# Sums of squares in four column groups, roots and inverses on 128 partitions, in a hybrid decoder step

## The reference, cut to what matters

```python
q = l2_normalize(q.reshape(n_b, t_len, H_C, DK)) * (DK ** -0.5)   # x * rsqrt(sum(x*x) + 1e-6)
k = l2_normalize(k.reshape(n_b, t_len, H_C, DK))
...
o, delta_new = gated_delta_rule(q, k, v, g, beta, delta_prev)      # chunks of tokens, four heads
o = rms_norm(o, o_norm_g) * silu(c_gate)
y_c = o.reshape(n_b, t_len, D_C)
x = x + einsum('bte,ed->btd', concatenate([y_a, y_b, y_c]), w_out)
x = x + hier_moe(rms_norm(x, norm2_g), ...)                        # 32 experts of 256
```

## Time and profile before

| | |
|---|---|
| runs | 720.87 us median of 3 (718.63, 720.87, 726.35) |
| span of the profiled execution | 720.5 us, 0.4 us under the median |
| its busy shares | PE 89%, PEld 64%, DVE 49%, ACT 28%, POOL 18% |
| chain that ended last | PE 68%, DMA 18%, DVE 8%, ACT 2%, issue 2% |
| mean granted TensorE clock | 0.971 |

### The profile page before, as it was taken

The page is one execution under the profiler, slowest core; times in us unless marked ns, Lnnn a source line. Parts: engine busy times, 40 slices in busy tenths (PEclk is TensorE's granted clock), DMA queues, the critical chain, the costliest instruction groups (busy, mean ns, idle before and its releaser), DMA issues.

```text
span 720.5 us, 12831 instructions
## 1 busy us (share of the span) xinstructions
PE 644.8 (89%) x4674; PEld 463.6 (64%) x4675; DVE 355.3 (49%) x705; ACT 200.9 (28%) x419; POOL 129.0 (18%) x226
## 2 busy tenths in 40 slices
PE   5998999999979998999999999787887799789885
PEld 4998998889869888894455655343343455455431
DVE  4657686879987748645765551111111112111237
ACT  6464366531432351234021201111111111101114
POOL 0010010200530010040011235311122223223110
PEclk9999999999989999999999979999999999999996
DMA  9232333233090000005961168999999999989836
GB/s 280 64 90 60 87 88 88 60 89 71 6 365 10 1 1 1 2 1 190 346 210 58 65 253 310 411 411 413 416 415 414 407 409 412 415 347 395 323 108 268
DMA packets 74792, 150.60 MB, mean 209 GB/s; under 512 B 14964, under 2 KB 51144, under 8 KB 66543
## 3 DMA queue, kind: packets, MB, share of 16 engines
q1 hardware_dynamic: 69167, 141.28, 53.1%
q0 software_dynamic: 5568, 8.54, 3.3%
HBM read 140.90 MB, written 18.20 MB: 221 GB/s over the span
## 4 chain that ended last, share of the span: by engine, by line
PE 68%; DMA 18%; DVE 8%; issue 2%; ACT 2%; SPq 0%; POOLq 0%; DVEq 0%; POOL 0%; ACTq 0%
PE ps L1899 21%; DMA wd<-w_down 17%; PE ps L2255 14%; PE ps L1994 8%; PE ps L2086 7%; DVE XX L1581 2%; PE ps L2207 2%; PE ps L2277 1%; PE ps L2296 1%; PE ps L2176 1%; PE ps L1912 1%; PE ps L1848 1%; DMA yk<-expert_rows 1%; PE ps L1988 1%; PE ps L2064 1%
## 5 line engine op out<-in xcount | busy, mean ns | idle before, releaser
L2255 PE MATMUL ps<-gu,xT 128*64 128x256 f32 x992 | 123.0, 392 | 35.2 <-DMA wd<-w_down 32.2
L1899 PE MATMUL ps<-hhi,whi 128*128 128x256 f32 (+1 forms) x416 | 121.1, 291 | 3.4 <-DVE wlo L1281 1.8
L2255 PEld LDWEIGHTS ps<-gu,xT 128*64 128x64 f32 x992 | 68.8, 139 | 85.4 <-issue 36.8
L1899 PE MATMUL ps<-hlo,whi 128*128 128x256 f32 (+1 forms) x416 | 118.8, 286 | 0.0
L1899 PE MATMUL ps<-hhi,wlo 128*128 128x256 f32 (+1 forms) x416 | 118.8, 286 | 0.0
L1760 DVE SCALAR_TENSOR_TENSOR gact<-gth,ps 128x128 f32<-128x128 f32 x32 | 9.2, 288 | 156.5 <-ACT gth L1013 156.5
L1899 PEld LDWEIGHTS ps<-hhi,whi 128*128 128x128 f32 x416 | 79.7, 192 | 7.9 <-issue 4.6
L1899 PEld LDWEIGHTS ps<-hhi,wlo 128*128 128x128 f32 x416 | 80.1, 192 | 0.0
L1899 PEld LDWEIGHTS ps<-hlo,whi 128*128 128x128 f32 x416 | 79.8, 192 | 0.0
L2255 PE MATMUL ps<-wd,aT 128*64 128x512 f32 x248 | 59.4, 600 | 0.0
L2086 PE MATMUL ps<-wout,yT 128*128 128x512 f32 x128 | 59.1, 602 | 0.0
(11 more groups left out here) (405 smaller groups left out, 979.9 us busy)
## 6 DMA issues: line engine op xcount, KB each, us to landing
gu<-w_gate SPq DMA_DIRECT2D x31, 1024.0 KB, 11.3
gu<-w_up SPq DMA_DIRECT2D x31, 1024.0 KB, 14.4
wd<-w_down SPq DMA_DIRECT2D x31, 1024.0 KB, 17.2
wraw<-w_in SPq DMA_DIRECT2D x26, 512.0 KB, 3.8
wout<-w_out SPq DMA_DIRECT2D x1, 4096.0 KB
yk<-expert_rows SPq DMA_DIRECT2D x8, 512.0 KB, 6.9
x<-x_prompt SPq DMA_DIRECT2D x4, 512.0 KB, 7.1
s<-state_delta SPq DMA_DIRECT2D x4, 512.0 KB, 6.2
```

The costliest lines, as they stand in the source:

```text
L1899: last = mm(ps[:, 2 * (n % 2) + half, 0:hi - lo], weights[:, c, :], h[:, c, lo:hi], start=c == 0 and j == 0, stop=c == KT - 1 and j == len ...
L2255: last = mm(ps[g * CAP:(g + 1) * CAP, bank, 0:width], left(c), right(c, g), start=c == 0, stop=c == steps - 1)
```

## The change

The sum over partitions is taken in quarters of the columns. Quarter g of a tile (136 columns, 130 for the outputs) goes to column group g, that is to PSUM partitions 32g to 32g+31, with a stationary operand of 128x32 that has ones in columns m and m+16. Each sum so stands twice in its group of 32 partitions, at m and at m+16. Root and inverse then run on 128 partitions and a quarter of the columns, and the split is one `scalar_tensor_tensor`: a column `low` (0 for the first 16 partitions of each 32, -1 for the others) leaves the rounded inverse in the first and makes the rest in the second. The spread picks a row and its rest with a 128x128 operand out of `quarter_sel`, one matmul for each quarter. The constants grow by 37 columns, which the same DMA loads; a fill of `norm` with zeros (line 1318) goes and a copy of 16 columns comes in its place.

```diff
-            return cst[:, C_COL + 7 - m:C_COL + 15 - m]
+            return cst[:, C_COL + 3 - m:C_COL + 35 - m]
+        def select_quarter(g, m):
+            return quarter_sel[:, 4 * g + m:4 * g + m + 1].broadcast_to([P, P])
...
-                copy(rn[:, 0, :], ps[0:8, 4, 0:HC], ACT.Sqrt, scale=0.25,
-                     bias=epsc[0:8, :]).then_inc(sums_ready, 1)
+                copy(rn[:, 0, :], ps[:, 4, 0:QC], ACT.Sqrt, scale=0.25, bias=epsc[:, :]).then_inc(sums_ready, 1)
...
-            link(nc.vector.memset(norm[:, :].bitcast(F32), 0.0))
+            link(nc.vector.tensor_copy(quarter_sel[:, :], cst[:, C_QUARTERS:C_QUARTERS + 16]))
...
                 link(nc.vector.reciprocal(rn[:, 1, :], rn[:, 0, :]))
-                link(nc.vector.tensor_copy(norm[0:8, :], rn[:, 1, :]))
-                nc.vector.tensor_tensor(norm[32:40, :], rn[:, 1, :], norm[0:8, :], ALU.subtract).then_inc(norms_ready, 1)
+                link(nc.vector.tensor_copy(norm[:, :], rn[:, 1, :]))
+                stt(out=norm[:, :], in0=norm[:, :], scalar=low, in1=rn[:, 1, :], op0=ALU.mult, op1=ALU.add).then_inc(norms_ready, 1)
...
-                for half in range(2):
-                    last = mm(ps[0:8, 4, 0:HC], column(j % 4 + 4 * half), sq[j % 2][:, half * HC:(half + 1) * HC],
-                              start=j % 4 == 0 and half == 0, stop=j % 4 == 3 and half == 1)
+                for g in range(4):
+                    last = mm(ps[32 * g:32 * g + 32, 4, 0:QC], column(j % 4), sq[j % 2][:, g * QC:(g + 1) * QC],
+                              start=j % 4 == 0, stop=j % 4 == 3)
...
-                for half in range(2):
-                    last = mm(ps[:, 6 + half, 0:HC], select(j % 4 + 4 * half), norm[:, :], start=True, stop=True)
+                for g in range(4):
+                    last = mm(ps[:, 6 + g // 2, g % 2 * QC:(g % 2 + 1) * QC], select_quarter(g, j % 4), norm[:, :], start=True,
+                              stop=True)
```

More of the change, by code:

```diff
@@ L42 @@
 HC = CV // 2
+QC = CV // 4
+QT = T // 4
 EPS = 1e-6
@@ L75 @@
 C_COL = C_LM + 128 * LEVELS
-C_REV = C_COL + 16
+C_REV = C_COL + 36
 C_GIR = C_REV + NE
@@ L84 @@
 C_PICK = C_CAPS + MORE
-C_END = C_PICK + 8
+C_QUARTERS = C_PICK + 8
+C_LOW = C_QUARTERS + 16
+C_END = C_LOW + 1
 def constants():
@@ L99, in constants @@
         c[:, C_LM + n * P:C_LM + (n + 1) * P] = (i // 2 == j // 2) & (i % 2 == 1) & (j % 2 == 0)
-    c[:, C_COL + 7] = 1.0
+    c[:, C_COL + 3] = 1.0
+    c[:, C_COL + 3 + 16] = 1.0
     c[:, C_REV:C_REV + NE] = 99 - np.arange(NE)
@@ L111, in constants @@
     c[:, C_PICK:C_PICK + 8] = p[:, None] % 32 == np.arange(8)
+    for g in range(4):
+        for r in range(4):
+            c[:, C_QUARTERS + 4 * g + r] = (p // 32 == g) & (p % 16 == r)
+    c[:, C_LOW] = -1.0 * (p % 32 >= 16)
     return c
@@ L190, in build @@
         sel = keep("sel", [40, 8], F32R)
-        norm = keep("norm", [40, HC], F32R)
+        quarter_sel = keep("quarter_sel", [P, 16], F32R)
+        norm = keep("norm", [P, QC], F32R)
         rowsr = keep("rowsr", [40, SEQ], F32R)
@@ L248, in build @@
         uas = first("uas", [P, 2, NS, WA])
-        rn = first("rn", [8, 2, HC])
+        rn = first("rn", [P, 2, QC])
         delta = Region(K4, K5 - 1920)
@@ L274, in build @@
         osq = [mix(f"osq{s}", [P, T]) for s in range(2)]
-        rno = mix("rno", [8, 2, HT])
+        rno = mix("rno", [P, 2, QT])
         rowq2 = mix("rowq2", [27, CQ * P])
@@ L344, in column @@
         def column(m):
-            return cst[:, C_COL + 7 - m:C_COL + 15 - m]
+            return cst[:, C_COL + 3 - m:C_COL + 35 - m]
         def select(m):
             return sel[:, m:m + 1].broadcast_to([40, P])
+        def select_quarter(g, m):
+            return quarter_sel[:, 4 * g + m:4 * g + m + 1].broadcast_to([P, P])
+        low = cst[:, C_LOW:C_LOW + 1]
         def rows(i):
@@ L917, in _ @@
             act.wait_ge(onorm_done, H)
-            copy(rno[:, 0, :], ps[0:8, 1, 0:HT], ACT.Sqrt, scale=1.0 / P,
-                 bias=epsc[0:8, :]).then_inc(oroot_ready, 1)
+            copy(rno[:, 0, :], ps[:, 1, 0:QT], ACT.Sqrt, scale=1.0 / P, bias=epsc[:, :]).then_inc(oroot_ready, 1)
             act.wait_ge(rows_turned, 4)
@@ L1602, in _ @@
             link(nc.vector.reciprocal(rno[:, 1, :], rno[:, 0, :]))
-            link(nc.vector.tensor_copy(norm[0:8, 0:HT], rno[:, 1, :]))
-            tt(norm[32:40, 0:HT], rno[:, 1, :], norm[0:8, 0:HT], ALU.subtract).then_inc(onorm_ready, 1)
+            link(nc.vector.tensor_copy(norm[:, 0:QT], rno[:, 1, :]))
+            stt(out=norm[:, 0:QT], in0=norm[:, 0:QT], scalar=low, in1=rno[:, 1, :], op0=ALU.mult, op1=ALU.add).then_inc(onorm_ready, 1)
             vec.wait_ge(ds_vec, 8)
@@ L2106, in _ @@
                 pe.wait_ge(osq_ready, n + 1)
-                for half in range(2):
-                    last = mm(ps[0:8, 1, 0:HT], column(n + H * half), osq[n % 2][:, half * HT:(half + 1) * HT],
-                              start=n == 0 and half == 0, stop=n == H - 1 and half == 1)
+                for g in range(4):
+                    last = mm(ps[32 * g:32 * g + 32, 1, 0:QT], column(n), osq[n % 2][:, g * QT:(g + 1) * QT], start=n == 0,
+                              stop=n == H - 1)
                 last.then_inc(onorm_done, 1)
@@ L2128, in _ @@
                     pe.wait_ge(oscaled, n - 1)
-                for half in range(2):
-                    last = mm(ps[:, (0, 4)[n % 2] + half, 0:HT], select(n + H * half), norm[:, 0:HT], start=True, stop=True)
+                for g in range(4):
+                    last = mm(ps[:, (0, 4)[n % 2] + g // 2, g % 2 * QT:(g % 2 + 1) * QT], select_quarter(g, n), norm[:, 0:QT],
+                              start=True, stop=True)
                 last.then_inc(onorm_done, 1)
```

## The result

| | median (us) | range, runs | ratio to before, 95% |
|---|---|---|---|
| before | 721.66 | 718.63 to 726.35, 4 | |
| changed | 710.50 | 709.71 to 710.75, 4 | 0.9852 [0.982, 0.9883] |

The change makes the kernel 1.5% faster, 11.2 us by the medians. The profiled execution of the changed kernel took 710.75 us with a span of 708.9. An execution thus takes 1.8 us more than its span.

The account below looks back on a forecast made before the run. TensorE was taken to bound the projection. Savings of 5.7 us there and 1.9 in the norm of the outputs, 7.6 in all, took 720.5 to 712.9, given as 713.2 us; range 711.0 to 718.0.

Parts of the forecast that it names:

- What bounds the kernel: Projection, 73 to 196 us: TensorE alone, busy 35.00 of 35 us, so sums and spreads between tiles are paid in full.
- The new sum: Sums of squares: eight passes of 136 columns in four column groups take 0.37 us instead of 1.02, saving 0.65 each.
- The new spread: Spreads in the projection: four 128-row matmuls take 0.47 us instead of 0.59, saving 0.12 alone, 0.62 together with a sum.
- The ways in and out: Around a spread: leaving and re-entering the full array costs 0.35 us, expected to go with all 128 rows in use.
- Cover by DVE: End of projection: DVE's inversion saves 0.8 us, and its 1.16 us wait at the last gate remains as cover.
- The outputs: Norm of the outputs: first spread 1.3 us earlier, outer products a further 0.6, together 1.9 us saved.
- the term for the half-clock stretches: Between stages: granted clock may fall elsewhere, a microsecond or two either way; inside the gain-caught-later rival, 715.2 us, chance 0.14.
- narrow float32r: Rival, spreads: float32r at 136 columns runs like plain float32, a spread costs 0.93 us; time 718.9 us, chance 0.12.
- the ways don't stay: Rival, spreads: the ways in and out stay, a spread costs 0.82 us; time 717.6 us, chance 0.10.
- the loads don't hide behind the streaming: Rival, spreads: four weight loads hide behind streaming, 0.25 us in all; time 711.4 us, chance 0.06.
- the groups share: Rival, sums: column groups do not overlap, a sum takes 1.76 us instead of 1.02; time 728.6 us, chance 0.03.
- the gain isn't caught by DVE: Rival, projection: DVE uses only its 2.88 us idle and the shorter inversion, projection gives 3.7; 715.2 us, chance 0.14.

Follow-up runs that it names:

- the two experiments in which the trace names DVE as what it waited for: Kernel before with only the spreads' operands brought to 128 rows, 718.75 us; changed kernel with each reciprocal of q and k done twice, 711.43 us.
- the 128-row experiment: Kernel before with only the spreads' operands brought from 40 to 128 rows, sums, roots and inverses as they were: 718.75 us, ratio 0.9961.

## Why the prediction was wrong by a little, step by step

**What bounds the kernel** was right: TensorE in the projection, busy 35.00 of 35 us before and after, so that every sum and spread is paid in full.

**The new sum**, 0.37 predicted, 0.37 measured. The estimate from the experts' four groups holds: eight passes in two rounds. A repeat behind another sum costs 0.23, the estimate without the ways 0.25.

**The new spread** is the term that was mis-sized. A tile with a spread alone takes 158.89 - 152.71 = 6.18 where it took 6.37, so a spread saves 0.19 and not 0.12; at the fifth of the eight spreads, where the step was 6.48 before, it saves 0.30. The projection gave 6.14 instead of 5.7. Both prices were off. The old one was read too low: the 28.89 us of 240 matmuls hold a first tile of 5.86, behind other matmuls, and run to the end of the last one; between its like a tile takes 5.74 from start to start and not 5.78, so the old spread cost 0.63 and not 0.59. The new one costs 6.18 - 5.74 = 0.44 and not 0.47. Its weight loads start 0.11 apart, close to the 0.106 of the earlier trace rows. The second matmul starts only 0.06 behind the first, which makes the 0.40 from start to start above, but most of that is given back where the second projection matmul behind a spread starts 0.17 behind the first and not 0.12. The row of the routing has the same cheap first step, 0.03, and 0.11 for each later one; its mean of 0.106 hides that. Behind a sum the spread saved what was predicted: 7.39 - 6.77 = 0.62. The 81 ns of the Trainium skill ("TensorE: Matmul & The Clock Gate", "Back-to-back issue gap") would make 0.32 of four, as an estimate; the run has 0.44, so the measured 0.11 a load was the better price.

**The ways in and out** go, as predicted, but not wholly: the first projection matmul behind a spread lasts 0.33, where 0.28 was foreseen. The 128-row operands alone take 6.37 - 6.01 = 0.36 from a spread, the 0.35 read from the earlier trace rows. The rule of the Trainium skill ("TensorEngine Tiling (Array Packing)", "Key Properties"), that a change of the tiling mode drains TensorE, agrees with this.

**Cover by DVE.** The inversion got shorter by 2.6 - 1.6 = 1.0 us, 0.8 predicted (6.1 ns a column for the reciprocal, not 5.3), and the wait at the last gate was 1.05 where 1.16 was foreseen. But the statement that those 1.16 are the cover was wrong: the nearer edge is the spread of the fifth tile, with 0.45 after the change. In the kernel before it had none. There the chain that ended last and DVE's timeline have

```profile
164.96 0.07 issue
165.02 0.49 PE ps L1923 x2
...
164.16 0.71 DVE L1423 SCALAR_TENSOR_TENSOR cv<-cv,ps 128x544 f32<-128x544 f32 x1
```

The spread starts 0.15 behind the end of DVE's multiplication at 164.87, as it does in the two experiments in which the trace names DVE as what it waited for. This is the 0.11 by which the step with the fifth spread was longer, 6.48 for 6.37. The prediction looked for waits of DVE, and this is a wait for DVE.

**The outputs**, 1.9 predicted, 2.18 measured. The first spread moved by 1.63, since besides the sums (3.73 to 2.35) ACT's shorter root, 0.37 instead of 0.47, stands ahead of its copy of the turned rows, and the first spread no longer waits for DVE's inversion. Before, it did:

```profile
334.18 0.29 PEld L2130 LDWEIGHTS ps<-norm,sel 40*128 40x128 f32 x2 [0.27 <-DVE norm L1604]
```

The rest of the 2.18 is 0.55, predicted 0.6. PE no longer holds DVE, as predicted. One sign was wrong: the outer products are still released by ACT's copy, which ends at 331.52, 0.1 after DVE's last multiplication.

**The time and the range.** The terms were 0.7 us too small in all (0.4 in the spreads, 0.3 in the outputs), and that leaves 712.5, inside the range. The step that failed is the term for the half-clock stretches. The prediction has it among the rivals, "Where PE idles between stages the granted clock may also fall at other points than now, a microsecond or two either way", but prices it with one value above the forecast and gives it nothing in the lower end of a range that "reaches from 711.0 to 718.0". As a scatter about every case it reaches well below 711: the same kernel was timed from 708.01 to 715.73, the stretch up to the eighth tile alone differing by 3.0 us and the one up to the first expert by 2.7. That the first four fell just below 711.0 is in part luck, since the two repeats of the same kernel have medians of 714.74 and 711.34, both inside the range. Within 1% had more of the chance than faster, though 8.3 us alone are 1.15%; the forecast itself was 1.06%. The note that the profiled execution lies 0.4 under the median set a span against times; it had 722.46 us of its own, 0.8 over the median of the four. That error cost little here, and 712.9 with 0.4 is 713.3, not 713.2.

**The rivals** fell by the trace: narrow float32r runs at the price of its loads, the ways don't stay, the loads don't hide behind the streaming (0.11 from one to the next), the groups share, and the gain isn't caught by DVE. This last one was nearer than its 0.14 says: the 128-row experiment is that case, and without the shorter inversion the change would have lost 0.58.

## What to carry to other kernels

A wait that is cover must be looked for at every place where the slower engine hands something back, not only at the last one: here the bound would have moved at a spread that waits for the multiplication of the tile before, with 0.45 us to spare against 1.05 at the end, and with none before the change. Such a place shows on the engine that waits, in one step that is longer than its like (6.48 among four of 6.37). Narrow matmuls in a row paid for their weight loads here, 0.11 us each. The price of a plain tile is read from start to start between its like, not from the mean of a stretch whose ends cost extra. And where stages differ by a microsecond or more between executions of one kernel, the range of a forecast needs that scatter on both sides, and a gain is better read from the stages that the change touches than from the whole time.

## What was not expected of the hardware

A reciprocal on DVE costs by its columns, whether on 128 partitions or 8: 1001 ns for 136 columns, 966 for 130 and 1772 for 260 on 128 partitions, 1836 for 272 on 8.

TensorE's clock falls to 1.2 GHz in stretches that differ between executions of one kernel, even where PE is busy throughout (20 to 32 us: 12.00 of 12 at 0.86 and at 1.00). In these two places each is worth 1.1 to 1.7 us: 53.18, 54.72 and 56.24 us for the same work up to the eighth tile, 90.76 to 95.21 from the outer products to the first expert. What decides in which execution a dip comes was not settled.
